# Hyena long convolution: result rows to every sixteenth partition of the inverse's buffer, with their transfers issued by GpSimd

## The reference, cut to what matters

```
s = (v * x1)                                   # 1024 tokens x 1024 channels
g = hyena_filter(...)                          # two-sided filter, 2048 x 1024, normalised
y = irfft(rfft(s, n=2048) * rfft(g, n=2048))[:, :1024]
y = (y + s * skip) * x0
return y @ w_out + b_out
```

## Time and profile before

| what | value |
|---|---|
| median of three runs | 2461.24 us (2459.37 to 2461.28) |
| the profiled execution | 2460.01 us, of which its span is 2458.2 us |
| TensorE busy (matmul) | 2365.6 us, 96% |
| VectorE, ScalarE, GpSimd busy | 1107.8, 605.4, 646.3 us |
| the result transfers YB<-yi | 16, 512 KB each, on ScalarE's queue |
| the loads gr<-g, bs<-s, kf<-kc | 16 each; 512, 512 and 224 KB, on SyncE's queue |

### The profile page before, as it was taken

One profiled execution on the slowest core, in us unless ns is written; L12 is line 12 of the kernel. 1 busy time (PEld: TensorE's weight loads), 2 busy tenths in 40 slices (PEclk: granted clock), 3 DMA queues, 4 the chain that ended last, 5 costly groups with the idle time before them and its releaser, 6 DMA issues.

```text
span 2458.2 us, 29269 instructions
## 1 busy us (share of the span) xinstructions
PE 2365.6 (96%) x11692; PEld 1900.3 (77%) x11692; DVE 1107.8 (45%) x1131; ACT 605.4 (25%) x672; POOL 646.3 (26%) x362
## 2 busy tenths in 40 slices
PE   7999998799999999999997999999999999999996
PEld 5766772378888888888886888989897877778885
DVE  6765445352662055413366827363543024500533
ACT  4333313422110010001123626262633011111011
POOL 2221210123333233333342122222222233323321
PEclk9999999899999999999998999999999999999997
DMA  4143239512221223112111202020214221112231
GB/s 155 51 124 127 89 123 342 208 35 84 96 85 43 85 77 102 51 43 69 51 59 36 103 27 77 26 77 26 77 33 172 102 77 56 56 43 67 96 120 68
DMA packets 75331, 211.51 MB, mean 86 GB/s; under 512 B 22006, under 2 KB 25912, under 8 KB 75002
## 3 DMA queue, kind: packets, MB, share of 16 engines
q1 hardware_dynamic: 64794, 172.72, 21.5%
q10 hardware_dynamic: 10464, 37.75, 4.1%
HBM read 165.36 MB, written 40.37 MB: 84 GB/s over the span
## 4 chain that ended last, share of the span: by engine, by line
PE 75%; DVE 3%; ACT 1%; issue 0%; ACTq 0%; DVEq 0%
PE ps L1205 63%; PE ps L538 5%; DVE T L1855 1%; PE ps L1479 1%; PE ps L585 1%; PE ps L604 1%; PE ps L605 1%; PE ps L567 1%; PE ps L606 1%; PE ps L1227 1%; DVE XN L1885 0%; PE ps L1236 0%; PE ps L504 0%; DVE X L2179 0%; DVE H L1878 0%; PE ps L523 0%
## 5 line engine op out<-in xcount | busy, mean ns | idle before, releaser
L1205 PE MATMUL ps<-H,whi 128*128 128x512 f32 x4000 | 1083.9, 393 | 20.6 <-DVE H L1922 10.1
L1205 PEld LDWEIGHTS ps<-H,whi 128*128 128x128 f32 x4000 | 750.9, 189 | 198.1 <-issue 28.9
L1155 POOL CAST whi<-wraw 128x1024 fp32r<-128x1024 f32 x174 | 182.3, 1048 | 1690.4 <-PE ps L1205 842.8
L1205 PE MATMUL ps<-H,wlo 128*128 128x512 f32 x2000 | 618.2, 390 | 0.0
L1157 POOL TENSOR_TENSOR wlo<-wraw,whi 128x1024 fp32r<-128x1024 f32 x178 | 452.2, 2540 | 53.2 <-ACT whi L672 39.3
L1205 PEld LDWEIGHTS ps<-H,wlo 128*128 128x128 f32 x2000 | 376.8, 188 | 79.3
L1205 PE MATMUL ps<-A,whi 128*128 128x512 f32 x1472 | 395.8, 391 | 9.3 <-DVE A L2211 4.9
L1205 PEld LDWEIGHTS ps<-A,whi 128*128 128x128 f32 x1472 | 276.9, 188 | 68.3 <-issue 5.3
L1205 PE MATMUL ps<-A,wlo 128*128 128x512 f32 x736 | 227.4, 390 | 0.0
L1205 PEld LDWEIGHTS ps<-A,wlo 128*128 128x128 f32 x736 | 138.7, 188 | 29.0
L2095 DVE TENSOR_TENSOR T<-ps,T 128x1024 f32<-128x1024 f32 x22 | 26.9, 1224 | 155.8 <-PE ps L1205 155.8
(11 more groups left out here) (336 smaller groups left out, 2307.3 us busy)
## 6 DMA issues: line engine op xcount, KB each, us to landing
wraw<-in_panels SPq DMA_DIRECT2D x181, 512.0 KB, 3.6
mw<-in_modp SPq DMA_DIRECT2D x24, 512.0 KB, 3.6
g<-gsp SPq DMA_DIRECT2D x16, 512.0 KB, 3.7
gr<-g SPq DMA_DIRECT2D x16, 512.0 KB, 12.6
bs<-s SPq DMA_DIRECT2D x16, 512.0 KB, 12.2
YB<-yi ACTq DMA_DIRECT2D x16, 512.0 KB
X<-in_xT SPq DMA_DIRECT2D x4, 1024.0 KB, 7.1
s<-sa SPq DMA_DIRECT2D x8, 512.0 KB, 2.7
```

The source lines that it names most:

```text
L1155: nc.gpsimd.tensor_copy(whi[:, s, :, :], wraw[:, s, :, :]).then_inc(hi_made, 1)
L1205: last = mm(p[:, c * step:(c + 1) * step], w[:, ws, k, :], operand(act, a, k, c * step, step), start=(q == 0 and w is whi and a == 0), sto ...
```

## The change

The eight partitions of group g become g, g + 16, ..., g + 112, so a group's rows are spread over all 128 partitions, and successive groups lie beside each other. The constants of the inverse are loaded in the new order, again with four transfers. The issue of each result transfer goes from ScalarE's list to GpSimd's, where sixteen waits and issues now stand between the last panel split of the first part and the wait for the last three transfers. The semaphores of the results are new ones; the three that they shared with the loads of X now serve the ring of `kf`.

```
-        kf_in = [(sem(f"kf_in{u}"), 0) for u in range(3)] + [(g1_out[u], 16 * (N2 // 2 + N2 // 4)) for u in range(2)]
+        kf_in = [(x_in[1 + u], 16) for u in range(3)] + [(g1_out[u], 16 * (N2 // 2 + N2 // 4)) for u in range(2)]
...
-        y_out = x_in[1:4]
+        y_out = [sem(f"y_out{u}") for u in range(3)]
...
-            return y_out[g % 3], 16 + 16 * (g // 3 + 1)
+            return y_out[g % 3], 16 * (g // 3 + 1)
...
-            return slice(g % 4 + 32 * (g // 4), g % 4 + 32 * (g // 4) + 29, 4)
+            return slice(g, P - GROUPS + 1 + g, GROUPS)
...
-            for a in range(0, P, 32):
-                sp.dma_start(cst[a:a + 32, CST["idft"]:CST["idft"] + HALF],
-                             d["cst"][a:a + 32, CST["idft"]:CST["idft"] + HALF].rearrange("(b r) c -> r b c", r=8)
+            rows = d["cst"][:, CST["idft"]:CST["idft"] + HALF].rearrange("(g r) c -> r g c", r=P // GROUPS)
+            for a in range(0, P // GROUPS, 2):
+                sp.dma_start(cst[a * GROUPS:(a + 2) * GROUPS, CST["idft"]:CST["idft"] + HALF], rows[a:a + 2, :, :]
                              ).then_inc(const_in, 16)
...
             rest(1, N0["wout"] // 2)
+            for g in range(GROUPS):
+                pool.wait_ge(spec_ev, g + 1)
+                pool.dma_start(YB[y_rows(g), :, :], yi[g % 3][:, :]).then_inc(y_stored(g)[0], 16)
             for g in range(GROUPS - 3, GROUPS):
                 pool.wait_ge(*y_stored(g))
...
                     act.wait_ge(*y_stored(g - 3))
                 A_(yi[g % 3][:, :], ps[Y_SLOT][:, :], ACT.Copy).then_inc(spec_ev, 1)
-                act.wait_ge(spec_ev, g + 1)
-                act.dma_start(YB[y_rows(g), :, :], yi[g % 3][:, :]).then_inc(y_stored(g)[0], 16)
```

## The result

The changed kernel takes 2495.39 us (median of four runs, 2493.96 to 2499.91); the kernel before took 2460.3 us beside it (four runs, 2458.94 to 2461.28). The ratio is 1.0146, with a 95% interval of 1.0129 to 1.0164: 35 us slower. The prediction said 2484.7 us. The direction and the place of the loss were right, its size came out a third too small.

What follows compares the result with a forecast made beforehand. The prediction took transfers on eight shared engines to bound the spectral stage; +27.7 us cadence, -6.2 for block moves and +2 at the end made +23.5, so 2484.7 us, own range 2470 to 2498.

Steps and rivals of the forecast that it cites:

- The stage is bound by transfers, TensorE's floor is 4.29 us a group: Spectral stage: a group takes 5.29 us on average, 4.29 undisturbed; the missing 1.0 us is waiting for data.
- ScalarE's and GpSimd's issues, the constants: 0: Spectral stage and inverse: moving sixteen issues to GpSimd and loading the inverse's constants in another order cost 0.
- A transfer to rows sixteen apart, alone: 4.13 us: Spectral stage's result transfer: 524.3 kB at 127 GB/s, the slowest measured stretch; 7.14 us a group with the loads.
- upper bound of 4.94 us: Result's part per group if two engines halve each other's rate, 2 x 2.47 us; 7.95 us with the loads.
- other value, 4.8 us: Result transfer through four ports at about 109 GB/s by the skill's table: 7.8 us a group, near 2496 us.
- Loads and result add up: 3.01 + result: Spectral stage: eight shared engines carry 3.01 us of loads plus the result's time per group and set the pace.
- all sixteen engines: Rival, spectral stage: GpSimd's result transfers spread over all engines, 4.25 us a group, under TensorE's floor; 2443 us, chance 0.14.
- Three block moves: -6.2 us: Spectral stage: rows change blocks after every four groups; transfers overlap there, half a transfer back each, 3 x 2.07 us.
- The tail: +2 us: From the last yi copy to the inverse, 8.5 us before: queued transfers could make it 12.4; +2 us taken.
- Everything after is only shifted: Sign for the forecast: what follows the spectral stage only starts later.
- the signs that the prediction asked for: Spectral stage: yi copies 6.5 to 7.5 us apart, result packets over 200 ns, loads over 15 us, transfer waits.
- full collision: Rival, spectral stage: 7.95 us a group, +39.9 us, and +4 us for the last three transfers; 2505 us, chance 0.20.

Runs made afterwards that it cites:

- the first series: Kernel before plus transfers at its very end, nothing else moving: eight of 512 KB from a 128-partition tile to rows four apart, issued by ScalarE; 184 GB/s.
- the halves kernel: Against the kernel before: GpSimd issues, rows four apart, even groups into partitions 0 to 63, odd ones into 64 to 127; 2446.46 us, ratio 0.9939.
- the second series: Kernel before plus transfers at its very end, nothing else moving: eight of 512 KB from a 128-partition tile to rows sixteen apart, issued by ScalarE; 103 GB/s.

## Why the prediction was right in direction and short in size

- **The stage is bound by transfers, TensorE's floor is 4.29 us a group.** Right. Better engines and places brought it to 4.47 us and the kernel to 2446.5.
- **ScalarE's and GpSimd's issues, the constants: 0.** Right for the issues in sum: issuer moved, rows kept, ratio 1.0 within 0.1%. GpSimd's issue takes 0.58 us, below the bounds of 0.62 to 2.54. The new order of the constants isn't in that run; in the changed kernel's trace the inverse waits for YB<-yi, not for them.
- **A transfer to rows sixteen apart, alone: 4.13 us.** This is the mis-sized term. I took 127 GB/s from the slowest stretch of before; measured alone it is 103 GB/s, 5.09 us. It also lay outside the upper bound of 4.94 us: that bound let two engines halve each other's rate, but began from 2.47 us, the price of undisturbed ones. The prediction's other value, 4.8 us, was nearer. As an image of the new place the 127 GB/s of the earlier trace rows had nothing to say: the old rows, four apart, reach 184 GB/s alone in the first series, though that series writes only into partitions 0 to 63 and the stretch wrote into 96 to 127. The half isn't what made it 127: the halves kernel, whose engines and halves fit, moves 134 GB/s from 444 to 448 us, where results move alone too. The cause stays open.
- **Loads and result add up: 3.01 + result.** This part held where the engines are the same as before: 3.01 + 5.09 = 8.10 us, measured 8.21 with ScalarE issuing. The reason given was that eight engines do both one after the other. That run can't tell it from the other one, that the loads must pass the same place. The changed kernel can: with results on both sets of engines, an engine would carry 3.01 + 5.09 / 2 = 5.56 us a group, but 7.61 is measured, and the loads' packets take 241 ns in place of 138 with all sixteen engines busy. So in the changed kernel the place is shared, and not only the engines as the prediction had it.
- **GpSimd's other engines.** The rival "all sixteen engines" had the mechanism right and its effect wrong. With the rows sixteen apart it gives back 9 us (2504.32 to 2495.39, 8.21 to 7.61 us a group), with rows four apart nothing, and only with the matching half its full gain. It asked whether the place was free; it wasn't. The forecast left this out: 7.14 against 7.61 us is two errors that partly cancel, +0.96 us for the transfer (and 0.11 that the sum misses), -0.60 for the engines. That 2495.39 us lies inside the range of 2470 to 2498 is partly luck: the same rows on the eight engines that the forecast assumed take 2504.32, outside it.
- **Three block moves: -6.2 us.** Not borne out in the stage: with ScalarE issuing nothing falls below the plain sum of 8.10 us. The effect as such is there, but smaller. In the second series the rate is 107 GB/s before the move from the fourth to the fifth transfer (2490 to 2506 us), 135 around it (2506 to 2509) and 103 after it (2509 to 2524). An estimate from these rates is 0.9 us saved a move, where the prediction gave 2.07. The cadence cost +34.7 us, where the prediction's terms made +27.7 - 6.2 = +21.5.
- **The tail: +2 us.** It was +0.6 (9.15 us from the last issue to the inverse, 8.55 before).
- **Everything after is only shifted.** Right, but for the 2.0 us that it was shorter, less than the spread of the four runs.

Most of the signs that the prediction asked for came: loads over 15 us to land, ScalarE's copy waiting for the transfer, the wait before the inverse grown from 9.67 to 10.99 us. A mean packet of the results over 200 ns came only with the 4-byte packets left out (369 ns; with them 0.381 x 480 / 1114 = 164). The cadence of 7.61 us lay just outside the 6.5 to 7.5 given. It was nearest to the full collision (7.95 us, 2505 us), whose time is also that of the new rows without the change of engines (2504.3).

## What to carry to other kernels

Before spreading rows over the partitions, ask which places they share on the way in, and with whom: a transfer into a narrow place runs at that place's rate with however many engines, and it slows every load that must pass there, so the loss appears as a wait for data that nobody touched. When one transfer uses half of the engines, the issuing engine decides which half; here placing each group's rows to suit its engines gained 0.6%, the opposite placement lost 0.4%, on the same instructions. A price that the trace doesn't show is best had from a series of such transfers alone; the slowest stretch of the old kernel isn't it.

## What the runs showed that was not expected

- GpSimd's queue carries 4352 packets for 16 transfers, 272 each, of which 128 hold data; the other 144 have 4 bytes. ScalarE's transfers have about eight such packets each (62 in some eight transfers of the first series). With the old rows GpSimd's issuing as a whole, these packets included, costs nothing measurable (ratio 1.0).
- Source rows sixteen apart limit a transfer as destination rows do (107 and 104 GB/s by the packets, against 141).
- The same program with only the two halves of the destination exchanged differs by 24 us, 1% of the time; in the profiled executions 21.9 us of it lie ahead of the inverse's start (454.48 and 476.36 us).
